# A recurrent layer's query norms on one core: turned queries squared with an accumulating output, in place of products with a column of ones

## What is computed

```
q = l2_normalize(split_heads(q, nh)) * GDN_DK ** -0.5      # tf * rsqrt(sum(tf * tf, -1) + 1e-6)
...
o = chunk_gated_delta_rule(q, k, v, g, beta).transpose(0, 2, 1, 3)
o = o * lax.rsqrt(jnp.mean(o * o, -1, keepdims=True) + NORM_EPS) * norm_g.astype(F32)
o = o * jax.nn.silu(z.astype(F32)).reshape(bsz, seq, nh, GDN_DV)
```

## Time and profile before

| | us |
|---|---|
| median of 3 executions | 1069.2 |
| their range | 1067.49 to 1074.75 |
| the profiled execution, its own time | 1066.15 |
| its span, first to last instruction | 1064.3 |
| TensorE busy in the span | 1031.1 |
| VectorE busy | 773.5 |
| ScalarE busy | 594.1 |

### The profile page before, as it was taken

One profiled execution on the slowest core, in us unless ns is written; L12 is line 12 of the kernel. 1 busy time (PEld: TensorE's weight loads), 2 busy tenths in 40 slices (PEclk: granted clock), 3 DMA queues, 4 the chain that ended last, 5 costly groups with the idle time before them and its releaser, 6 DMA issues.

```text
span 1064.3 us, 18722 instructions
## 1 busy us (share of the span) xinstructions
PE 1031.1 (97%) x7676; PEld 972.0 (91%) x7676; DVE 773.5 (73%) x1327; ACT 594.1 (56%) x1011; POOL 1.3 (0%) x13
## 2 busy tenths in 40 slices
PE   7999998999999999999999999999999999999997
PEld 7999997999999988899987899999899888999996
DVE  7999999799877778766777555555789666555555
ACT  5577455675555567653546545454655555454453
POOL 0000000000000000000000000000000000000000
PEclk9999999999999999999999999999999999999999
DMA  9996574477766523631233656656365336655511
GB/s 372 419 384 202 177 240 176 161 254 280 240 195 195 182 80 101 189 127 61 80 99 120 210 193 192 193 186 192 120 230 167 123 115 238 198 192 185 183 57 40
DMA packets 58021, 195.47 MB, mean 184 GB/s; under 512 B 10320, under 2 KB 10704, under 8 KB 57680
## 3 DMA queue, kind: packets, MB, share of 16 engines
q1 hardware_dynamic: 56784, 194.21, 53.9%
q10 hardware_dynamic: 1152, 0.07, 0.1%
HBM read 192.94 MB, written 1.31 MB: 183 GB/s over the span
## 4 chain that ended last, share of the span: by engine, by line
PE 80%; DVE 13%; ACT 4%; issue 1%; DMA 1%; SPq 0%; DVEq 0%; ACTq 0%
PE ps L553 71%; PE ps L852 3%; DVE lo L1710 2%; PE ps L636 2%; DVE B L2124 1%; DVE raw L1697 1%; ACT hi L1151 1%; DVE sm L1887 1%; PE ps L729 1%; DVE xa L1721 0%; PE ps L709 0%; DVE B L1778 0%; ACT B L1506 0%; DVE sm L1962 0%; DVE Z L2153 0%
## 5 line engine op out<-in xcount | busy, mean ns | idle before, releaser
L1710 DVE TENSOR_TENSOR lo<-raw,hi 128x1024 fp32r<-128x1024 f32 x311 | 377.5, 1221 | 125.2 <-ACT hi L1151 124.5
L553 PE MATMUL ps<-hh,hi 128*128 128x256 f32 x1568 | 442.7, 282 | 6.8 <-DVE hl L1755 3.1
L553 PE MATMUL ps<-hh,lo 128*128 128x256 f32 x1568 | 438.0, 279 | 0.0
L553 PE MATMUL ps<-hl,hi 128*128 128x256 f32 x1568 | 437.9, 279 | 0.0
L1151 ACT ACTIVATE hi<-raw 128x1024 fp32r<-128x1024 f32 x311 | 324.8, 1052 | 50.3 <-PE ps L553 50.2
L553 PEld LDWEIGHTS ps<-hh,hi 128*128 128x128 f32 x1568 | 294.9, 188 | 10.6 <-DVE lo L1710 3.4
L553 PEld LDWEIGHTS ps<-hl,hi 128*128 128x128 f32 x1568 | 295.0, 188 | 1.6
L553 PEld LDWEIGHTS ps<-hh,lo 128*128 128x128 f32 x1568 | 294.9, 188 | 0.0
L553 PE MATMUL ps<-hi,fh 128*128 128x512 f32 x192 | 76.3, 397 | 0.0
L553 PE MATMUL ps<-lo,fh 128*128 128x512 f32 x192 | 75.9, 395 | 0.0
L553 PE MATMUL ps<-hi,fl 128*128 128x512 f32 x192 | 75.7, 394 | 0.0
(11 more groups left out here) (279 smaller groups left out, 1236.9 us busy)
## 6 DMA issues: line engine op xcount, KB each, us to landing
raw<-in_w SPq DMA_DIRECT2D x359, 512.0 KB, 4.3
B<-in_t SPq DMA_DIRECT2D x2, 512.0 KB, 4.2
xa<-in_x SPq DMA_DIRECT2D x1, 1024.0 KB, 11.8
B<-in_r SPq DMA_DIRECT2D x1, 1024.0 KB, 6.4
out<-h SPq DMA_DIRECT2D x4, 256.0 KB, 2.0
cst<-in_c SPq DMA_DIRECT2D x1, 864.0 KB, 9.7
vec<-in_v SPq DMA_DIRECT2D x1, 328.5 KB, 8.1
between<-Z ACTq DMA_DIRECT2D x8, 8.0 KB, 1.5
```

The source lines that it names most:

```text
L553: m = g.matmul(o, l, r, start=first and n == 0, stop=last and n == 2, skip_group_check=True)
L1710: g.tensor_tensor(lo[:, j % SPLIT, :], raw[:, PLACE[j] % RAW, :], hi[:, j % SPLIT, :].bitcast(F), ALU.subtract).then_inc(*up("lo", j))
```

## The change

In `qsum(u)` TensorE now turns the four blocks of unsquared queries (128 channels by 128 tokens) into a whole bank, tokens on the partitions. ScalarE squares each turned block of 128x128 from PSUM, and the operation's accumulating output writes the sum over the free dimension, the channels, into its column of `qss`; the squares themselves go to `crow` and are not read. VectorE scales `qss` in place. ScalarE's square of 128x512 in `qk(u)` is gone. TensorE's turn of pair u waits for the silu of the queries, and for the squares of pair u - 1, which free bank 3.

```
             def qsum(u):
-                b = take_bank("qss", 3) if u == 3 else 3
+                b = take_bank("qsum", 3) if u == 3 else 3
                 if u < 3:
-                    s.wait_ge(*(at("qss", u - 1) if u else at("z", 3)))
-                s.wait_ge(*at("qsq", u))
+                    s.wait_ge(*(at("qsum", u - 1) if u else at("z", 3)))
+                s.wait_ge(*at("qsilu", 2 * u + 1))
                 for n in range(4):
-                    m = g.matmul(bank[b][:, n:n + 1], qsq[:, u % 2, n % 2, n // 2 * P:n // 2 * P + P], ones[:, 2, 0:1],
-                                 start=n == 0, stop=True, skip_group_check=True)
-                m.then_inc(*up("qss_mm", u))
+                    m = g.transpose(bank[b][:, n * P:n * P + P], qb[:, 2 * u + n % 2, n // 2 * P:n // 2 * P + P], ident)
+                m.then_inc(*up("qturn_mm", u))
...
             def qk(u):
                 take_bank()
-                s.wait_ge(*at("qsilu", 2 * u + 1))
-                if u > 1:
-                    s.wait_ge(*at("qss_mm", u - 2))
-                g.activation(qsq[:, u % 2], qb[:, 2 * u:2 * u + 2, :], ACT.Square).then_inc(*up("qsq", u))
 
             def qsum(u):
-                if u == 3:
-                    take_bank()
+                b = take_bank() if u == 3 else 3
+                s.wait_ge(*at("qturn_mm", u))
+                for n in range(4):
+                    g.activation(crow[:, n * P:n * P + P], bank[b][:, n * P:n * P + P], ACT.Square,
+                                 accum_out=qss[:, n // 2, 2 * u + n % 2:2 * u + n % 2 + 1]).then_inc(
+                                     *up("qsum", (u, n) if n < 3 else u))
...
             def qsum(u):
-                b, hs = take_bank() if u == 3 else 3, slice(2 * u, 2 * u + 2)
-                s.wait_ge(*at("qss_mm", u))
-                g.tensor_scalar(qss[:, :, hs], bank[b][:, 0:4].rearrange("p (c n) -> p c n", c=2), P * NORM_EPS,
-                                P * NORM_EPS * NORM_EPS, ALU.mult, ALU.add).then_inc(*up("qss", u))
+                hs = slice(2 * u, 2 * u + 2)
+                if u == 3:
+                    take_bank()
+                s.wait_ge(*at("qsum", u))
+                g.tensor_scalar(qss[:, :, hs], qss[:, :, hs], P * NORM_EPS, P * NORM_EPS * NORM_EPS, ALU.mult,
+                                ALU.add).then_inc(*up("qss", u))
```

More of the change, by code:

```diff
@@ L257 @@
           "rule_pe": ("kturn_mm", "kk", "turnT_mm", "P_mm", "T_mm", "TT_mm", "rv_mm", "vn_mm", "state_mm",
-                      "carry_mm", "qss_mm", "qk", "o_mm", "gturn_mm"),
-          "rule_act": ("ksq", "kd", "klen", "turnT", "rv", "state", "qsq", "osq", "osd", "gh"),
+                      "carry_mm", "qturn_mm", "qk", "o_mm", "gturn_mm"),
+          "rule_act": ("ksq", "kd", "klen", "turnT", "rv", "state", "qsum", "osq", "osd", "gh"),
           "rule_dve": ("kss", "ks", "low", "inv", "T", "TT", "P", "wd", "vn", "r1", "qss", "qdec", "attn", "oss", "orms", "ocf",
@@ L428, in program @@
         lm = [Z[:, a:a + 1024].rearrange("p (c i s) -> p c i s", c=2, i=4) for a in (3072, 4096)]
-        qsq = crow[:, :].rearrange("p (u i s) -> p u i s", u=2, i=2)
         kss, ks, qss, mo, ocf = (smv(o) for o in (176, 192, 208, 224, 240))
```

## The result

The kernel after takes 1072.58 us (median of 22 runs, 1069.91 to 1076.71), beside 1070.26 us for 22 runs of the kernel before. The ratio is 1.0027 (95% interval 1.0016 to 1.0038): slower by 2.9 us (1.7 to 4.1), or 2.3 by the medians, with 2.45 forecast. The profiled execution lasts 1075.54 us with a span of 1073.7, 9.4 us more than before's. That is more than the difference of the medians, and the granted clock says why: its mean is 0.988 there and 0.996 in before's profiled execution. Read in stretches of 1 us, after's trace has six falls of the clock that cost 1.7 us each (from 18, 178, 188, 396, 536 and 547 us on); before's has one such fall (from 376 us on); in both the clock is also down in the last 5 us, where TensorE has nothing to do.

A forecast was written before the change was run, and what follows sets the result against it. TensorE, 97% busy, was taken as the bound nearly everywhere, but it waits for ScalarE and VectorE around the change. 0.52 + 0.47 + 1.46 = +2.45 us: profiled 1066.15 becomes 1068.6, the median 1071.6; range 1067.0 to 1076.5.

The forecast's parts named there:

- bound of "same": Whole kernel: about 1%, 10.7 us, is what a measurement can tell; chance of landing inside it 0.94.
- Price of a square: ScalarE's accumulating square of 128x128 with its read: 0.31 us each, 1.33 us for the four of one pair.
- the lower end, 0.20: A square at 0.20 us, its read costing nothing: each of the three delays loses 0.44, +1.1 us in all.
- "No overlap": Rival: each accumulating square on ScalarE is served without overlap, 0.58 us; +5.7 us, 1074.9; chance 0.10.
- Terms 1 and 2: ScalarE's query squares delay its square of pair 1's output, +0.52 us, and VectorE's convolution of tile 23, +0.47 us.
- Term 3: Query squares delay ScalarE's table load and square of pair 2, so the turn of its gated output waits: +1.46 us.
- The waits: TensorE at pair 2's scores, the residual's second half and the turn of pair 2's gated output: 2.2, 2.5, 1.9 us.
- Step 0: First query sum, at 515.57 us: ScalarE's squares fit with 0.5 us to spare; cost nothing, TensorE 0.46 us early.
- The clock: Rival: the granted clock falls at the three longer waits, 1.7 us each; +7.6 us, 1076.8; chance 0.15.
- Turns as the cause of the falls: Argument that turns do not keep TensorE's clock up, against swapping products for turns ahead of a wait; no separate size.
- TensorE alone: Rival: only TensorE's time counts, so its four gains reach the end; -1.84 us, 1067.4; chance 0.08.
- The table load: ScalarE's load of the square root's table: 1.41 us from its start to the next square, no 2.66 us cost.

## Why the prediction was right, and where its parts were off

- **The total**: +2.45 forecast, +2.9 by the ratio measured, within the bound of "same". It is right, but made of other parts: 2.0 us of late instructions (rest 1.7 in the kernel after with two falls, 1.84 in its repetition with one, 1.98 filled with none), and a share of the clock.
- **Price of a square**: mis-sized, 0.31 us taken, 0.25 measured. The overlap of the read was right in kind; the lower end, 0.20, was as near as my value. With 0.25 each term loses 0.24 us and the sum of the forecast is +1.7, beside 1.98 measured. "No overlap" falls with it.
- **Terms 1 and 2**: +0.99 forecast, +0.63 measured at a whole clock; 0.51 with 0.25-us squares. The scores of pair 2 are 536.89 - 515.44 = 21.45 us into the stage, 21.12 before: term 1 is +0.33. That the squares are paid in full is shown by the doubled squares. That what comes off TensorE ahead of a wait only lengthens the wait is true of the change, but not in general: with the turns alone the scores of pair 2 start 20.22 us into the stage, 0.90 earlier than before, because ScalarE and VectorE, which they wait for, start earlier too.
- **Term 3**: +1.46 forecast, +1.35 measured. Its mechanism, the table load behind the query squares, is shown by moving the load: the wait of 1.62 us is gone.
- **The waits**: 2.2, 2.5 and 1.9 forecast, 2.00, 2.26 and 1.62 measured, short by 0.20 to 0.28, which is about what a step's cheaper squares make.
- **Step 0**: cost nothing, as forecast; no wait stands there.
- **The clock**, the step that failed: I let the longer waits cost themselves alone and gave the clock a chance of 0.15 as a rival. It fell behind two of the three in after's profiled execution and behind one in the repetition's, 1.7 us each as I had priced it. Over runs, filling the waits gives back 2.6 ± 1.3 us, while the same filling gives the kernel before nothing. I had named the fall around the wait of 2.05 us and still let the 1.56-us wait, at a clock of 1.00, outweigh it: the two waits that I forecast at 2.2 and 2.5 us lay above 2.05.
- **Turns as the cause of the falls**: not the query turns, since with products in their place the clock fell the same; the other turns about the second wait weren't changed.
- **TensorE alone** (-1.84) was nearly true of the turns alone (-1.35), and of the change only where its squares are put into ScalarE's idle time (-1.2, -0.96).
- **The table load**: 1.41 and 1.40 us from its start to the next square, as in the earlier trace rows. By the Trainium skill ("ScalarE: Activation LUTs", What ACT_TABLE_LOAD costs) it would be 2.66 us; no row here shows the drain in it.

That the total came out near 2.45 is partly luck: the squares were 0.7 us cheaper in sum, and the clock, put at nothing, took about as much (2.9 - 1.98 = 0.9 us by the total) or more (2.6 by the filling). The shares can't be fixed to better than 1.3 us.

Open: how often the clock falls in an execution, with one profile of each kernel, and what beside its length makes a wait one with a fall. In the stage, waits of 1.82, 1.98, 2.00, 2.26 and 2.34 us had a fall behind them, and one of 1.97 and another of 2.26 had none. Elsewhere in the program the same holds over the 14 profiles: the wait of some 2.03 us between 376 and 382 us had a fall in ten of them and the one of 1.7 us near 185 in three, while one of 2.00 to 2.07 us near 412 had none in the eleven that have it. Open too: the three filled versions on one chip have totals 1.5 to 1.8 us lower, against the kernel before, than their stages say (+0.3 for +1.98, -2.8 for -0.96, -1.3 for +0.27). That the kernel before loses more to the clock in other executions than in its profiled one would explain it, but its own filling gained nothing.

## What to carry to other kernels

Moving work to an engine that is busy 56% of the time is free only where that engine stands idle: read its timeline at each place, and look at what is queued behind the new work, table loads first. A place of an instruction in its own engine's order (an independent load ahead of a wait) was worth more here than the instruction's price. Where a kernel lives at the full clock, count a wait of TensorE of about 2 us as the wait and a possible fall (here 1.7 us), and try it with idle products in the gap before judging an edit.

## What the runs showed of the hardware

- Run to run, this kernel's time follows the mean granted clock: 0.988 goes with 1074.6 to 1075.5 us, 0.993 with 1071.1 to 1072.1. The 22 runs of the kernel after spread over 6.8 us, and most of that goes with the clock.
- A fall from 2.4 to 1.2 GHz behind a wait of TensorE of 2.00 us and one of 2.26 us cost 1.7 us each, and such falls also stood behind waits of 1.82 and, elsewhere in the program, 1.7 us; with idle products in the gaps the clock stayed at 1.00, and did also behind waits of 0.78 and 1.56 us. A wait of this length need not bring a fall: one of 2.26 us had none when the kernel was run again.
- An accumulating square of 128x128 from PSUM costs 0.25 us from start to start, less than its own 0.277 us (median) of duration, with its read of 0.21 us, as the operations by line show for the kernel after:

```profile
L1563 ACT ACTIVATE crow<-ps x16: 268/277/303, 520.7 to 558.1; 128x128 f32<-128x128 f32 x16
L1563 ACT ACTIVATION_READ_ACCUMULATOR crow<-ps x16: 194/212/237, 520.9 to 558.3; 128x1 f32 x16
```
